# Paired experts: weight loads round eight slots instead of six, and ScalarE's two short copies ahead of the second up slot's rounding

## The reference

```python
logits = h @ moe_router                      # 256 tokens, 8 experts
top, idx = lax.top_k(logits, 2)
weight = softmax(top)
for each expert e:                           # w1, w3: 1024 x 3584, w2: 3584 x 1024
    hidden = silu(h_e @ w1[e]) * (h_e @ w3[e])
    y[tokens of e] += weight * (hidden @ w2[e])
x = x + gate * y
```

## Time and profile before

| | us |
|---|---|
| median of 3 runs | 2489.4 |
| lowest, highest | 2487.48, 2495.14 |
| profiled execution | 2496.13 |
| its span | 2494.3 |
| the paired experts in it | 575 to 1562 |

### The profile page before, as it was taken

How to read it: one execution, slowest core, us unless ns; L and a number is a source line. 1 busy time by engine, 2 the same in 40 slices (tenths; PEclk the granted TensorE clock), 3 DMA queues, 4 the chain that set the end, 5 groups by cost and what they waited for, 6 DMA issues and landing times.

```text
span 2494.3 us, 36105 instructions
## 1 busy us (share of the span) xinstructions
PE 2365.2 (95%) x14484; PEld 1922.5 (77%) x14484; DVE 1477.3 (59%) x1843; ACT 970.3 (39%) x1149; POOL 44.8 (2%) x37
## 2 busy tenths in 40 slices
PE   5999999998999999989999998999999999999999
PEld 4889998876566565656665665779899999997998
DVE  5835885764444454444544444375489887873665
ACT  3214434113434444343434434222434456653332
POOL 0100001000000000000000000010000000000000
PEclk9989999999999999999999999999999999999999
DMA  9845894746989999989989999230488543432452
GB/s 369 330 152 203 358 364 179 304 152 262 366 349 366 368 364 359 364 348 369 363 338 382 362 374 371 107 118 1 154 330 360 210 169 136 149 139 101 155 184 100
DMA packets 90428, 656.78 MB, mean 263 GB/s; under 512 B 10033, under 2 KB 10289, under 8 KB 10801
## 3 DMA queue, kind: packets, MB, share of 16 engines
q1 hardware_dynamic: 80928, 589.34, 61.2%
q10 hardware_dynamic: 9360, 65.52, 6.4%
HBM read 653.76 MB, written 1.05 MB: 263 GB/s over the span
## 4 chain that ended last, share of the span: by engine, by line
PE 78%; DMA 9%; DVE 6%; issue 3%; ACT 3%; ACTq 0%; SPq 0%; DVEq 0%
PE bank L1392 77%; DMA ring<-stream_dram 9%; DVE work L2274 1%; DVE ring_rounded L2262 1%; ACT hT L1064 1%; DVE ff_hid_rounded L2262 1%; DVE rstd L2322 0%; PE bank L1936 0%; DVE xT L2268 0%; ACT ff_hid_rounded L1070 0%; DVE ring L2274 0%; PE bank L1772 0%; DVE ff_mid L2268 0%; ACT work_rounded L1038 0%; DVE yT L2268 0%
## 5 line engine op out<-in xcount | busy, mean ns | idle before, releaser
L2262 DVE TENSOR_TENSOR ring_rounded<-ring,work_rounded 128x2048 fp32r<-128x2048 f32 x264 | 606.4, 2298 | 461.6 <-ACT work_rounded L1045 347.7
L1392 PE MATMUL bank<-work_rounded,proj_rounded 128*128 128x512 f32 x896 | 310.2, 418 | 1.5 <-DVE ring_rounded L2262 1.5
L1392 PE MATMUL bank<-h_heads_rounded,work_rounded 128*128 128x256 f32 x1344 | 278.9, 280 | 0.0
L1392 PE MATMUL bank<-yT_rounded,ring_rounded 128*128 128x256 f32 x960 | 273.6, 285 | 0.0
L1038 ACT ACTIVATE work_rounded<-ring 128x2048 fp32r<-128x2048 f32 x112 | 214.7, 1918 | 131.5 <-DMA ring<-stream_dram 131.0
L1392 PE MATMUL bank<-hT,ring 128*128 128x256 f32 x1088 | 242.9, 383 | 2.0 <-ACT hT L926 2.0
L1392 PEld LDWEIGHTS bank<-hT,ring 128*128 128x128 f32 x1088 | 207.5, 192 | 37.7 <-issue 9.9
L1392 PEld LDWEIGHTS bank<-h_heads_rounded,work_rounded 128*128 128x128 f32 x1344 | 220.6, 189 | 3.0 <-issue 2.9
L1045 ACT ACTIVATE work_rounded<-ring 128x2048 fp32r<-128x2048 f32 x56 | 107.2, 1914 | 286.9 <-DMA ring<-stream_dram 281.5
L1392 PEld LDWEIGHTS bank<-work_rounded,proj_rounded 128*128 128x128 f32 x896 | 177.1, 198 | 42.4 <-issue 2.8
L1392 PE MATMUL bank<-ring,proj 128*64 128x512 f32 x896 | 201.8, 592 | 0.0
(11 more groups left out here) (329 smaller groups left out, 4161.7 us busy)
## 6 DMA issues: line engine op xcount, KB each, us to landing
ring<-stream_dram SPq DMA_DIRECT2D x561, 1024.0 KB, 6.9
work<-stream_dram ACTq DMA_DIRECT2D x56, 1024.0 KB, 9.1
params<-params_dram ACTq DMA_DIRECT2D x1, 1728.5 KB, 28.9
consts<-consts_dram ACTq DMA_DIRECT2D x1, 1568.0 KB, 37.7
cond<-cond_dram ACTq DMA_DIRECT2D x2, 512.0 KB, 3.7
xT<-x_dram ACTq DMA_DIRECT2D x1, 1024.0 KB, 10.1
out_dram<-xT SPq DMA_DIRECT2D x1, 1024.0 KB, 3.9
consts<-consts_dram ACTq DMA_DIRECT2D x1, 577.0 KB, 32.2
```

Source lines behind the costliest of these rows:

```text
L1392: return pe.matmul(o, lhsT=a, rhs=b, start=start, stop=stop, skip_group_check=True)
L2262: return dve.tensor_tensor(o, a, b, op)
```

## The change

In the paired experts loads go round eight places (`PAIR_RING`). Six are those of `ring`, two more lie in `work`, behind the rounded buffers; to make room there, `back_pick`, which is used only in `experts_again`, moves onto the place of `many_pick`. The eight places have semaphores of their own (`pair_arrived`), so the counts of `weights_here` behind the stage are lower by the 56 rounds that are left out (`rounds_at`). A load of the stage waits for the slot eight before it. And on ScalarE `few_up_of(s)` and `hid_high_of(s)` now stand between the roundings of the next step's first and second up slot. The order of loads and of all other work is the same. The diff, cut to its core:

```diff
+PAIR_RING = RING + 2
@@ the work buffer
-        back_pick = take(NT * P).rearrange("p (t m) -> p t m", t=NT)
+        assert moe_n + 8 * SLOT <= work_n
+        more_slots, more_slots_r = ([w[:, moe_n + (6 + a) * SLOT:moe_n + (7 + a) * SLOT] for a in range(2)]
+                                    for w in (work, work_r))
+        back_pick = many_pick
@@ which place, which semaphore
+        pair_arrived = [sem(f"pair_arrived{i}") for i in range(PAIR_RING)]
         def pair_here(s, what, half=0):
-            at = moe_first + pair_slot(s, what) + half
-            return weights_here[at % RING], 16 * (at // RING + 1)
+            n = pair_slot(s, what) + half
+            return pair_arrived[n % PAIR_RING], 16 * (n // PAIR_RING + 1)
-        def pair_ring(s, what, half=0):
-            return (moe_first + pair_slot(s, what) + half) % RING
+        def pair_ring(s, what, half=0, rounded=False):
+            i = (pair_slot(s, what) + half) % PAIR_RING
+            if i >= RING:
+                return (more_slots_r if rounded else more_slots)[i - RING]
+            return (ring_r if rounded else ring)[:, (moe_first + i) % RING, :]
+        def rounds_at(at):
+            return at // RING + 1 - (MOE_CHUNKS * 3 // RING if at >= moe_first + 3 * MOE_CHUNKS else 0)
@@ SP, load_experts
-                    if n >= RING:
-                        sp.wait_ge(weights_used, moe_first + n - RING + 1)
+                    if n >= PAIR_RING:
+                        sp.wait_ge(weights_used, moe_first + n - PAIR_RING + 1)
@@ ScalarE, paired_experts
                     silu_of_many(s)
                     if s + 1 < PAIR_STEPS:
-                        for half in range(2):
-                            up_high_of(s + 1, half)
+                        up_high_of(s + 1, 0)
                     few_up_of(s)
                     hid_high_of(s)
+                    if s + 1 < PAIR_STEPS:
+                        up_high_of(s + 1, 1)
```

More of the change, by code:

```diff
@@ L728, in expert_slot @@
                     n = pair_slot(s, what) + half
-                    if n >= RING:
-                        sp.wait_ge(weights_used, moe_first + n - RING + 1)
+                    if n >= PAIR_RING:
+                        sp.wait_ge(weights_used, moe_first + n - PAIR_RING + 1)
                     part = 3 * c + (2 if what.endswith("down") else half)
-                    sp.dma_start(ring[:, (moe_first + n) % RING, :],
+                    sp.dma_start(pair_ring(s, what, half),
                                  stream_in[bass.ds(first_of[e] + part, 1)].rearrange("a p n -> p (a n)"))\
-                      .then_inc(weights_here[(moe_first + n) % RING], 16)
+                      .then_inc(pair_arrived[n % PAIR_RING], 16)
                 for s in range(PAIR_STEPS):
@@ L890, in attention_high @@
                 at = place[f"in{n}"] + s
-                act.wait_ge(weights_here[at % RING], 16 * (at // RING + 1))
+                act.wait_ge(weights_here[at % RING], 16 * rounds_at(at))
                 if s >= 4:
@@ L1037, in up_high_of @@
                         act.wait_ge(*pair_used(s - 2, "many", half))
-                    act.activation(up_high[s % 2][half], ring[:, pair_ring(s, "many", half), :], ACT.Copy)\
+                    act.activation(up_high[s % 2][half], pair_ring(s, "many", half), ACT.Copy)\
                        .then_inc(many_up_high, 1)
@@ L1044, in down_high_of @@
                         act.wait_ge(*pair_used(s - 2, "many_down"))
-                    act.activation(down_high[s % 2], ring[:, pair_ring(s, "many_down"), :], ACT.Copy)\
+                    act.activation(down_high[s % 2], pair_ring(s, "many_down"), ACT.Copy)\
                        .then_inc(many_down_high, 1)
@@ L1313, in high @@
                     at = 3 * odd + w + 2
-                    rounds = (first + at) // RING + 1
+                    rounds = rounds_at(first + at)
                     if isinstance(c, int):
@@ L1394, in arrive @@
             def arrive(at, i=None):
-                rounds = at // RING + 1
+                rounds = rounds_at(at)
                 pe.wait_ge(weights_here[at % RING], 16 * rounds if i is None else i * 16 + 16 * rounds)
@@ L1921, in many_up @@
                         low, high = (w.rearrange("p (k n) -> p k n", k=4)
-                                     for w in (ring_r[:, pair_ring(s, "many", half), :], up_high[s % 2][half]))
+                                     for w in (pair_ring(s, "many", half, True), up_high[s % 2][half]))
                         for k in range(4):
@@ L1948, in many_down @@
                             high, low = (w[:, j * D + b * 512:j * D + b * 512 + 512]
-                                         for w in (down_high[s % 2], ring_r[:, pair_ring(s, "many_down"), :]))
+                                         for w in (down_high[s % 2], pair_ring(s, "many_down", 0, True)))
                             mm(bank(b), hid_high, high, c == 0 and j == 0, False)
@@ L1963, in few_up_products @@
                         pe.wait_ge(*pair_here(s, "few", half))
-                        w = ring[:, pair_ring(s, "few", half), :].rearrange("p (k n) -> p k n", k=4)
+                        w = pair_ring(s, "few", half).rearrange("p (k n) -> p k n", k=4)
                         for k in range(4):
@@ L1982, in few_down @@
                         pe.wait_ge(few_outs, p)
-                    w = ring[:, pair_ring(s, "few_down"), :]
+                    w = pair_ring(s, "few_down")
                     for b in range(2):
@@ L2708, in up_low_of @@
                 def up_low_of(s, half):
-                    at = pair_ring(s, "many", half)
                     dve.wait_ge(many_up_high, 2 * s + half + 1)
-                    tt(ring_r[:, at, :], ring[:, at, :], f32(up_high[s % 2][half]), ALU.subtract).then_inc(many_up_low, 1)
+                    tt(pair_ring(s, "many", half, True), pair_ring(s, "many", half), f32(up_high[s % 2][half]), ALU.subtract).then_inc(many_up_low, 1)
                 def down_low_of(s):
-                    at = pair_ring(s, "many_down")
                     dve.wait_ge(many_down_high, s + 1)
-                    tt(ring_r[:, at, :], ring[:, at, :], f32(down_high[s % 2]), ALU.subtract).then_inc(many_down_low, 1)
+                    tt(pair_ring(s, "many_down", 0, True), pair_ring(s, "many_down"), f32(down_high[s % 2]), ALU.subtract).then_inc(many_down_low, 1)
                 def hidden_of_few(s):
```

## The result

The changed kernel takes 2415.4 us (median of 4 runs, 2414.48 to 2416.2) against 2488.4 us (median of 4) for the kernel before: 73 us less, a ratio of 0.9706 with a 95% interval of 0.968 to 0.9731. Forecast were 2422 us and a range of 2402 to 2465. The profiled execution took 2416.2 us with a span of 2414.4 us, 79.9 us less than that of before, whose profiled execution was 7.7 us above the median of its own runs.

What follows compares the result with a forecast made beforehand. TensorE was taken as the bound, losing 87 of 953 us to late loads. Plain steps 461, side-work steps 353, short-turn steps 63 and 9 left over make 886 us, gain 67: 2422 us, range 2402 to 2465.

Steps and rivals of the forecast that it cites:

- The bound and the place of the loss: Paired experts: TensorE bounds; 87 us of 953 us lost where late-issued loads pass through ScalarE and VectorE to TensorE.
- TensorE's floor: TensorE's time over the 55 step intervals if it waits for nothing: plain steps, gathers, scatters and short turns, 866 us.
- The rate of the transfers: Loads in the paired experts with eight slots: 410 GB/s taken, from the stage's first 25 us, rate divided by share.
- The plain step: A paired-expert step without side work: TensorE needs 15.0 us, the transfers at 410 GB/s 15.35 us; 30 such steps counted.
- The 9 us set down for waits and low clock that remain: Allowance in the stage's sum for remaining waits and low clock, a tenth of the 87 us lost.
- ScalarE's order: Two short copies ahead of the second up slot's rounding: costs nothing; gain counted with the slots, partly the same wait.
- T: The end of a step's up products on TensorE, just before the few expert's down product; other times count from it in us.
- The first (376 to 393 GB/s): Rival: transfers in the paired experts end the gain early, gain 23 to 47 us, 2442 to 2466 us; chance 0.21.
- the third: Rival: nothing to be had from the transfers, 362 GB/s is the limit itself; 2482 to 2494 us; chance 0.08.
- The second, the held-up rounding: Rival: second up slot's rounding, now behind the hidden block's, delays TensorE if slots still land late; 2512 us; chance 0.07.
- ScalarE's wait for the down slot under 60 us: Sign in the profile after: ScalarE's waits for the many expert's down slot fall from 281 us to under 60 us.
- A shorter longest wait of SP: Sign in the profile after: SP's longest wait for TensorE to give a slot back gets shorter; no size given.

## Why the prediction was right

**The bound and the place of the loss: right.** I had read from the chain and SP's waits that a load comes late because its slot comes back late, and that ScalarE and VectorE pass that on to TensorE. The releases worked out from one step said that two releases earlier are enough. The chain after the change and the run with the old order say so. That one is enough as well the prediction did not say; the same table of releases gave it before the run with seven slots, and that run bore it out.

**TensorE's floor: right in sum, with a wrong term.** 866 us were forecast and 875.2 measured. The third gather, that of the few expert's tokens in chunk 10, takes 3.55 us, not the 1.75 of the others. The timeline after the change shows its 32 pieces:

```profile
759.84 3.74 PE L1405 MATMUL bank<-h_heads,yT 128*128 128x64 f32 x32
763.38 0.48 PE L1405 MATMUL bank<-work_rounded,proj_rounded 128*128 128x512 f32 x1
```

I had taken one gather's row for all three kinds. Three of these add 5.4 us. The first step waits 3.7 us for VectorE (in the waits above; 4.0 us in the kernel before), and I had not counted it in the floor. 866 + 5.4 + 3.7 is 875.1 us. That this meets the measured time to 0.1 us is partly luck, for two more terms are missing that cancel: after that wait 5.4 us run at a granted clock of 0.50, which costs 2.7 us, and the first interval has no down product of the many expert, 12 products or 2.8 us less. The turn of the weights in chunk 7 was set too high besides: 0.8 us each, where the trace has about 0.45.

**The rate of the transfers: mis-sized.** The plain step was taken at 15.35 us from 410 GB/s; it takes 15.0 us, and the transfers can do it in 14.99 us, at 420 GB/s. That is 30 x 0.35 = 10 us too many. The quotient of a rate and its share was a poor measure of what the transfers can do; the slices of the burst, at 419 GB/s once it ran, were the good one. The 9 us set down for waits and low clock that remain were the 3.7 and 2.7 us of the first step, as above. Together: 886 - 10 - 9 + 5.4 + 3.7 = 876 us for 875 measured, with the 2.7 and 2.8 us left out on both sides. The terms that were too high outweighed the one too low, so the gain was 78 us in the stage and not 67. That is a miss of 11 us. The time of the kernel is off by 7 us only (2422 for 2415.4), and this is luck: the traced execution of the kernel before was 7.7 us above its median, so that between the medians the gain is 73 us.

**ScalarE's order: costs nothing, as said, and gains nothing.** With eight slots it is without effect; with six it is worth 36 us. That both edits remove partly the same wait was right, but the text did not say that the slots alone would remove all of it. It follows from the landing times that the text gives: a second up slot at T+0.7 is rounded long before the copy at T+5.3.

**The rivals.** The first (376 to 393 GB/s) falls by the run with eight slots and less work; so does the third. The second, the held-up rounding, needed late slots; with six slots and the new order the slots were late, and the kernel was 36 us faster, not slower. TensorE never waited for the second up slot's remainder.

**What would show it.** Idle time under 15 us: 9. Clock 0.99 or more: 0.99. Above 395 GB/s between 600 and 1450 us: 395, just on the mark, since TensorE asks for no more. ScalarE's wait for the down slot under 60 us: no, 113. I had the down slot landing at T+8.3 to T+10.9; in the trace after the change it lands at T+12.3 in the median, as a load now takes 7.9 us in the median from issue to landing. That is after ScalarE is free, but still before the T+13.1 that the prediction allows. The expectation confused a wait of ScalarE with one that matters. A shorter longest wait of SP: no, 11.3 us after 11.2.

## What to carry to other kernels

When loads are issued only as slots come back, write down for one unhindered step when each slot is given back and when it is wanted; the difference, less issue to landing, tells how many more slots remove the wait, and here it was one, not two. Once they are there, the order of short steps on the helping engines may be worth nothing; without them it was worth half of the gain here. To learn what the transfers can do, look at a stretch in which they are always queued, or take work from the other engine, and not at a mean over a stretch with waits.

## What the hardware showed that I had not expected

Less work on TensorE did not make the kernel faster, and probably made it slower. With 19% of its work in a step left out and six slots, the kernel went from 2491.6 to 2504.9 us (single runs), as the granted clock fell from 0.97 to 0.89 in the mean behind waits of up to 4.8 us; with products of constants in the place of what was left out it took 2459.2 us at a clock of 1.00. The Trainium skill (TensorE: Matmul & The Clock Gate, "HAM oscillation — how this bites in real kernels") tells of a kernel that goes back to the low clock at each wait for a transfer, and of idle gaps as the cause. These runs agree that idle time stands ahead of the lower clock, though it did not follow every wait. They also show that filling the gap can pay even when the filling is useless, and that it need not: in the kernel before, where TensorE was idle for 47 of 900 us (131 in the other) and the clock was at 0.97 already, a fill of 1.86 us a step cost 32 us.

And the transfers went at 420 GB/s for 800 us without a dip under 390, beside TensorE, ScalarE and VectorE at work on the same buffers, with loads of 1 MiB from one queue.
